# Sharing out layer 0's late w_ada tiles by stretch in a four-layer fp32 block

## The reference, cut to what matters

```python
mod = silu(c) @ w_ada[l] + b_ada[l]          # one row: 2048 x 6144 weights
shift, scale, gate = jnp.split(mod, 3, axis=-1)
h = _layernorm(x) * (1.0 + scale) + shift
u_f, z_f, cq, ckv, k_r, z_a = split(h @ w_in[l])
y_f = _fourier_mix(u_f, w_fmix[l]) * silu(z_f)
q  = _rmsnorm(cq, q_norm[l])  @ w_q_b[l]     # then rope
kv = _rmsnorm(ckv, kv_norm[l]) @ w_kv_b[l]
y_a = _mla_attention(q, k, v) * silu(z_a)
y = jnp.concatenate([y_f, y_a], axis=-1) @ w_out[l]
x = _layernorm(DEEPNORM_ALPHA * x + gate * y, ln_g[l], ln_b[l])
```

## Time and profile before

| what | us |
|---|---|
| median of three runs | 1583.13 |
| the profiled execution's own time | 1582.57 |
| its span in the trace | 1580.8 |
| PE busy / DVE busy / ACT busy | 1488.5 / 1067.2 / 704.5 |
| DMA, mean over the span | 218 GB/s |

### The profile page before, as it was taken

One profiled execution on the slowest core, in us unless ns is written; L12 is line 12 of the kernel. 1 busy time (PEld: TensorE's weight loads), 2 busy tenths in 40 slices (PEclk: granted clock), 3 DMA queues, 4 the chain that ended last, 5 costly groups with the idle time before them and its releaser, 6 DMA issues.

```text
span 1580.8 us, 25393 instructions
## 1 busy us (share of the span) xinstructions
PE 1488.5 (94%) x10111; PEld 1324.6 (84%) x10111; DVE 1067.2 (68%) x1723; ACT 704.5 (45%) x1199; POOL 40.7 (3%) x58
## 2 busy tenths in 40 slices
PE   5999999989949999999959999999998999999999
PEld 3678789987849788998849998889987998888987
DVE  3348588899887667577575683795655657766653
ACT  2334234344435445444335444454444546655442
POOL 3000000000000000000000000010000000000000
PEclk9999999999979999999979999999999999999999
DMA  9998788998827565776645554556665554444673
GB/s 356 406 406 318 260 305 322 351 356 333 330 76 261 189 204 175 251 256 200 198 132 185 175 163 145 146 178 199 186 197 150 162 160 122 126 115 129 186 217 104
DMA packets 101422, 345.04 MB, mean 218 GB/s; under 512 B 11216, under 2 KB 21684, under 8 KB 100536
## 3 DMA queue, kind: packets, MB, share of 16 engines
q1 hardware_dynamic: 96888, 327.42, 61.6%
q0 software_dynamic: 4416, 16.00, 3.0%
HBM read 341.17 MB, written 2.20 MB: 217 GB/s over the span
## 4 chain that ended last, share of the span: by engine, by line
PE 74%; DVE 12%; DMA 5%; ACT 4%; issue 3%; SPq 0%; DVEq 0%; ACTq 0%
PE PM L1453 62%; PE PB L1453 8%; DMA stg<-in_w_in 4%; DVE wlo L2128 2%; ACT whi L1816 2%; ACT AR L1816 1%; DVE X L2041 1%; DVE AC L2041 1%; PE PB L1667 1%; PE PB L1639 1%; DMA stg<-in_w_ada 1%; DVE SM L2381 1%; PE PB L1742 1%; DVE SM L2041 1%; PE PB L1714 1%
## 5 line engine op out<-in xcount | busy, mean ns | idle before, releaser
L2128 DVE TENSOR_TENSOR wlo<-stg,whi 128x1024 fp32r<-128x1024 f32 (+2 forms) x417 | 497.8, 1203 | 341.3 <-ACT whi L1816 339.3
L1816 ACT ACTIVATE whi<-stg 128x1024 fp32r<-128x1024 f32 (+2 forms) x417 | 429.4, 1038 | 435.4 <-PE PM L1453 340.7
L1453 PE MATMUL PM<-Hh,whi 128*128 128x256 f32 x1824 | 529.1, 293 | 12.8 <-DVE wlo L2128 8.8
L1453 PE MATMUL PM<-Hh,wlo 128*128 128x256 f32 x1776 | 501.2, 285 | 0.0
L1453 PE MATMUL PM<-Hl,whi 128*128 128x256 f32 x1824 | 497.6, 284 | 0.0
L1453 PEld LDWEIGHTS PM<-Hh,whi 128*128 128x128 f32 x1824 | 353.2, 194 | 32.1 <-issue 16.6
L1453 PEld LDWEIGHTS PM<-Hh,wlo 128*128 128x128 f32 x1776 | 344.0, 194 | 0.0
L1453 PEld LDWEIGHTS PM<-Hl,whi 128*128 128x128 f32 x1824 | 342.5, 193 | 0.8 <-issue 0.2
L1453 PE MATMUL PM<-whi,Hh 128*128 128x512 f32 (+1 forms) x576 | 223.9, 390 | 0.6 <-DVE wlo L2128 0.5
L1453 PE MATMUL PM<-wlo,Hh 128*128 128x512 f32 (+1 forms) x576 | 220.5, 384 | 0.0
L1453 PE MATMUL PM<-whi,Hl 128*128 128x512 f32 (+1 forms) x576 | 218.4, 384 | 0.0
(11 more groups left out here) (269 smaller groups left out, 1429.5 us busy)
## 6 DMA issues: line engine op xcount, KB each, us to landing
stg<-in_w_ada SPq DMA_DIRECT2D x163, 512.0 KB, 6.2
stg<-in_w_in SPq DMA_DIRECT2D x105, 512.0 KB, 5.3
stg<-in_even_w_in SPq DMA_DIRECT2D x80, 512.0 KB, 3.6
stg<-in_odd_w_in SPq DMA_DIRECT2D x72, 512.0 KB, 3.6
stg<-in_w_out SPq DMA_DIRECT2D x64, 512.0 KB, 4.2
stg<-in_even_w_out SPq DMA_DIRECT2D x32, 512.0 KB, 3.6
stg<-in_odd_w_out SPq DMA_DIRECT2D x32, 512.0 KB, 3.6
AR<-in_w_ada SPq DMA_DIRECT2D x29, 512.0 KB, 15.0
```

What stands on the lines that cost most here:

```text
L1453: return e.matmul(out, l, r, start=start, stop=stop, skip_group_check=True)
L1816: return e.activation(out, x, f, **k)
L2128: e.tensor_tensor(wlo[s["slot"]][:, :, 0:n], stg[s["slot"]][:, :, 0:n], whi[s["hi"]][:, :, 0:n].bitcast(F32), ALU.subtract).then_inc(SEM[" ...
```

## The change

`interleave` takes, in place of one pair (number of jobs, number of tiles), any number of such pairs, one for each stretch of the body, and shares the tiles evenly within each stretch. The rest of the body gets the rest of the tiles. Layer 0's call gets three pairs. The call of layer 1 is rewritten in the new form with its old numbers (70, 32).

```diff
-    def interleave(self, n0, extra, n1, some):
+    def interleave(self, n0, extra, *stretches):
         body = self.jobs[n0:]
         del self.jobs[n0:]
-        out, e = [], 0
-        for i, j in enumerate(body):
-            due = some * (i + 1) / n1 if i < n1 else some + (len(extra) - some) * (i + 1 - n1) / (len(body) - n1)
-            while e < len(extra) and e < due:
-                out.append(extra[e])
-                e += 1
-            out.append(j)
-        out += extra[e:]
+        rest = (len(body) - sum(n for n, _ in stretches), len(extra) - sum(m for _, m in stretches))
+        out, i, e = [], 0, 0
+        for n, m in stretches + (rest,):
+            for k in range(n):
+                out += extra[e + -(-m * k // n):e + -(-m * (k + 1) // n)]
+                out.append(body[i + k])
+            i, e = i + n, e + m
         self.jobs.extend(out)
...
-        self.interleave(n0, ex, 52, 76)
+        self.interleave(n0, ex, (8, 13), (12, 31), (32, 34))
...
-        self.interleave(n1 + 6, ex, 70, 32)
+        self.interleave(n1 + 6, ex, (70, 32))
```

## The result

The changed kernel is slower by a little: 1585.45 us (median of 20 runs, 1581.29 to 1588.45) against 1583.34 us (20 runs of the kernel before, 1580.55 to 1584.97). The ratio is 1.0017, with a 95% interval from 1.0011 to 1.0023. The forecast was 1.5 us faster, so its sign was wrong, by some 4 us in 1583. The time itself lies inside the forecast's range of 1576 to 1588.5.

What follows compares the result with a forecast made beforehand. PE, busy 94% of the span, was taken as the bound. A gain of 7.0 us in the gates and a loss of 5.5 before them gave -1.5 us, a median of 1581.6, range 1576 to 1588.5.

Steps and rivals of the forecast that it cites:

- Gates: Gates: PE's waits for DVE's `wlo`, 5.4 us, and 1.6 us of half clock behind them go, a gain of 7.0 us.
- Rate of the loads: w_q_b/w_kv_b stretch: loads run at 372 GB/s, the middle of three rates (406, 372, 339), with a backlog from about 177.
- the landing: End of the w_q_b/w_kv_b stretch: the first gate tile's load lands at 223.8, or at 220 or 228.3 by the other rates.
- my sum: w_q_b/w_kv_b stretch: 17.2 MB of loads from about 177 at 372 GB/s, first gate tile landing at 223.8, copy at 227.0.
- the loss in the w_q_b/w_kv_b stretch: w_q_b and w_kv_b groups: PE loses 5.5 us net, 4.7 by the middle load rate plus 0.8 for DVE's order.
- The 0.8 us: w_q_b/w_kv_b stretch: added to the loss for DVE standing in order behind small steps.
- 15 x 1.28 = 19.2 us: w_q_b/w_kv_b stretch: DVE's work on the tiles moved in, against 16.6 us idle, so at least 2.6 us late.
- B: Rival: in the w_kv_b groups DVE's copy comes so late that PE loses 12 against 7 gained: 1588.1, chance 0.20.
- A: Rival: the w_q_b/w_kv_b stretch takes the tiles in, loads near 400 GB/s, PE loses 0.1 to 1 us: 1576.7, chance 0.30.
- C: Rival: loads at about 355 GB/s, so loss and gain cancel: 1583.3, chance 0.12.
- D: Rival: the gates' waits stay in part, DVE's splits waiting for ACT; gain 3, loss 5.5: 1585.6, chance 0.06.
- the forecast's own 1580 to 1586: Whole kernel: the range of the likeliest case alone, around 1581.6, chance 0.32.

Runs made afterwards that it cites:

- only the gates were relieved: Against the kernel before, tiles taken out of the gates go to the output product, 33 there instead of 22: 1583.52 us, ratio 1.0006.
- half the bytes: Changed kernel with 29 w_ada tiles loaded only by half, DVE's instruction as long as before: 1583.99 us, 1.0006 of the kernel before.
- half the work: Changed kernel with whole loads, but DVE's instruction on the same w_ada tiles works on half the columns: 1581.88 us, 0.9999 of the kernel before.
- the second trace: The changed kernel run again with no edit, against the kernel before: 1585.63 us, ratio 1.0021.

## Why the prediction was wrong

**Gates: right, a little small.** The waits for `wlo` and the half clock behind them went entirely. The term was 7.0 us; it measured 7.9, 7.5, and 8.3 where only the gates were relieved. To this come 0.1 to 1.3 us in the output product, which I had at nothing.

**Rate of the loads: nearly right, the landing not.** I took 372 GB/s for a backlog from 177 on. It was 363 at a share of 0.97, which alone would have moved the landing by 1.1 us. But the backlog was not unbroken: from 200 to 210 it was 299 GB/s. From 196 to 210 SP waited 7.2 us for slots that DVE had yet to free, and 2.1 us for that of the bias tile, which POOL frees. SP issued the first gate tile's load at 221.18, it took 7.85 us, and it landed at 229.0 instead of 223.8 (1.1 of this comes from `u`). With half the bytes and with half the work it landed 44.5 and 45.1 us after the first w_q_b matmul, where my sum has 44.9 and the changed kernel 49.0. As a ceiling, the 358 GB/s that the prediction cites from the Trainium skill, "DMA: Bandwidth & Descriptors", section "Where 436 GB/s comes from", is passed by 392 with half the work on DVE, and by 406 in the earlier trace rows.

**The step that failed is the loss in the w_q_b/w_kv_b stretch: 5.5 us forecast, 9.7 measured (8.2 in the second trace).** Two things in it:

- *How late DVE comes.* I had bounded it twice, by DVE's work alone (at least 2.6 us) and by the loads alone (227.0 for the copy, 48.1 us after the first w_q_b matmul), and took the larger with 0.8 us for DVE's order. It was 53.0 and 52.2. The two runs with one side relieved came to 47.6 and 47.9: either limit alone gives about the number of my sum, and both together 5 us more. DVE waits for loads (8.1 us) while slots are few, and SP waits for slots while DVE works through copies, rope and softmax steps that stand in order between the tiles. The 0.8 us is the mis-sized term; by the copy it should have been 4.1 to 4.9. Of the kernel before's 13.6 us idle time of DVE up to the copy 5.5 were filled: busy time grew by 17.5 us and the copy came 12.0 later. 2.1 of these 17.5 are the instruction beside POOL's bias row, which I had moved ahead without a cost. My 15 x 1.28 = 19.2 us counted that bias tile too, which DVE never touches, and one tile that goes to `u`; between first w_q_b matmul and copy stand 13 tiles more.
- *Who feels it.* I costed the copies of the w_q_b groups at nothing, as the matmul that takes over their PSUM pair comes 10 us later. But the rope matmul that reads the copy stands right behind it on PE. That wait came first: 6.2 us, and the half clock behind it was 2.4 us where I had 0.8. Taking the wait away showed that the size of the loss hardly hangs on this choice.

**The `u` stretch.** "12 by the last `u` job, 13 after it" hid that the extra tile comes as early as the second job, ahead of a copy for which PE was already waiting 0.9 us. It costs 1.1 us (1.1 to 1.6 in the traces). I had given it no term.

**Rivals.** B came nearest by what happened: DVE's copies came so late that PE lost more in front than it won in the gates, and the first gate matmul came 12.7 us later, beyond the 10 that the prediction gave as B's sign. Its 12 us in front were too dear against 9.7 measured, its 339 GB/s were not seen, and its wait in the w_kv_b groups came already in the w_q_b groups. A is out. C is out as told, by a rate of 355 GB/s, though its canceling of loss and gain is not far from what was measured. D is out, as the gates' waits went whole; its 1585.6 us meets the 1585.45 measured by luck. By luck, too, the time lies within the forecast's own 1580 to 1586.

**What stays open.** The ledger gives +1.6 and +2.2 us, the timed runs 0.17% and 0.21%, which is 2.7 and 3.3 us (the medians differ by 2.1 and 3.9). The rest, about 1 us, may be more frequent long stays at the half clock behind the rope wait. The traces of both kernels show stays of 8.2 and 9.8 us in "rope to u", and two variants 11.5, but these are too few to show a difference. Open too is what the bias row on POOL costs: its 2.1 us on DVE stood ahead of the copy in the two relieved kernels as well, and no run was made without it.

## What to carry to other kernels

Idle time of an engine that works strictly in order is not capacity: of 13.6 us here 5.5 could be filled, since the engine's work and the loads that it frees slots for take turns. Where two limits hold each other up by a small pool of buffers, add what each costs, don't take the larger: either alone made the copy 6.6 and 6.9 us late, both together 12.0. Moved work has a cheap part and a dear part. Seven tiles out of the gates won nearly all that eleven did, at a sixth of the price in front, so try half of a redistribution first. And when work is put ahead of a copy, look for the first reader of that copy on the bounding engine, not for the next user of its buffer.

## What the runs showed of the hardware

The stretch from the first `u` to the first w_q_b matmul, in which PE hardly waits, repeats to 0.1 us in all fourteen traces (31.5 to 31.6). Behind PE's wait at 139 the stretch to the next mark lasts 6.5, 8.2, 9.8 or 11.5 us, in steps of 1.6 to 1.7, by how long the granted clock stays at half: it is 1.00 throughout in the trace with 6.5, and 0.50 from 142 to 150 in one with 11.5. Of 0.1 or 0.2% between two single profiled executions of this kernel, such steps can be the whole.

Beside POOL's instruction on the bias row (one partition by 1024 elements, 2.34 us) a DVE instruction that otherwise takes 0.41 us takes 2.52, in both traces of the changed kernel.
